# Sparse attention of a two-block network: constant products in front of the first scores, two weight splits moved into the pieces, and VectorE's work reordered

## The reference, cut to what matters

```python
q, k, v, qi, ki, wi = split(h @ w_in)                # 16 query heads, 4 key heads, index queries/keys
q, k, qi, ki = partial_rope(...)                      # rotary part: 16 of 64 features
score = einsum(relu(qi . ki), wi)                     # index scores, float32
sel = top_k(score where visible, 64)                  # 64 keys for each token
s = (q . k[sel]) / 8 ;  p = softmax(s) ;  o = p . v[sel]
x = x + o @ w_out
```

## Time and profile before

| what | value |
|---|---|
| median of 3 runs | 1656.52 us (1656.01 to 1660.21) |
| the profiled execution | 1656.1 us |
| its span | 1654.0 us |
| mean granted clock | 0.977 |
| busy share: PE, PEld, DVE, ACT | 97%, 93%, 61%, 46% |
| chain that ended last, by engine | PE 84%, DVE 8%, ACT 3%, DMA 3% |

### The profile page before, as it was taken

How to read it: one execution, slowest core, us unless ns; L and a number is a source line. 1 busy time by engine, 2 the same in 40 slices (tenths; PEclk the granted TensorE clock), 3 DMA queues, 4 the chain that set the end, 5 groups by cost and what they waited for, 6 DMA issues and landing times.

```text
span 1654.0 us, 30872 instructions
## 1 busy us (share of the span) xinstructions
PE 1606.0 (97%) x12599; PEld 1535.9 (93%) x12599; DVE 1004.1 (61%) x1233; ACT 764.8 (46%) x1009; POOL 23.1 (1%) x40
## 2 busy tenths in 40 slices
PE   7989999998999999999999999999999999999999
PEld 5868999998899998999987999989999898889998
DVE  6763665557666546656458666466664656676653
ACT  4333554446655534433436444344443435554443
POOL 0000000004000000000000000000000000000000
PEclk9956999999999999999999999999999999999999
DMA  5610666655056665555731557635566353146673
GB/s 167 166 61 1 178 190 189 184 169 156 27 169 190 193 186 166 178 166 178 199 117 52 180 177 202 178 102 180 177 203 178 102 181 100 57 142 185 201 210 96
DMA packets 339943, 253.62 MB, mean 153 GB/s; under 512 B 16302, under 2 KB 338700, under 8 KB 339868
## 3 DMA queue, kind: packets, MB, share of 16 engines
q1 hardware_dynamic: 337104, 250.00, 51.2%
q10 hardware_dynamic: 2764, 2.56, 0.6%
HBM read 250.51 MB, written 1.05 MB: 152 GB/s over the span
## 4 chain that ended last, share of the span: by engine, by line
PE 84%; DVE 8%; ACT 3%; DMA 3%; issue 1%; ACTq 0%; SPq 0%; DVEq 0%
PE acc L560 25%; PE acc L562 24%; PE acc L561 24%; DVE w_low L1774 2%; ACT w_high L1238 2%; PE acc L792 2%; PE spare L760 2%; PE acc L778 1%; PE acc L585 1%; DMA w_raw<-in_mlp_w_down_dram 1%; DMA w_raw<-in_ffn_w_dram 1%; DVE x_state L1984 1%; DVE xg_low L1818 1%; DVE evac_a L1982 1%; PE spare L623 1%
## 5 line engine op out<-in xcount | busy, mean ns | idle before, releaser
L1774 DVE TENSOR_TENSOR w_low<-w_raw,w_high 128x2048 fp32r<-128x2048 f32 (+2 forms) x218 | 519.5, 2383 | 373.2 <-ACT w_high L1238 373.1
L1238 ACT ACTIVATE w_high<-w_raw 128x2048 fp32r<-128x2048 f32 (+2 forms) x218 | 433.7, 1990 | 592.8 <-PE acc L562 553.9
L560 PE MATMUL acc<-xg_high,w_high 128*128 128x272 f32 (+2 forms) x2320 | 662.2, 285 | 7.7 <-DVE xg_low L1818 4.4
L562 PE MATMUL acc<-xg_high,w_low 128*128 128x272 f32 (+2 forms) x2320 | 654.7, 282 | 0.0
L561 PE MATMUL acc<-xg_low,w_high 128*128 128x272 f32 (+2 forms) x2320 | 654.7, 282 | 0.0
L560 PEld LDWEIGHTS acc<-xg_high,w_high 128*128 128x128 f32 (+1 forms) x2320 | 435.4, 188 | 19.4 <-issue 9.5
L561 PEld LDWEIGHTS acc<-xg_low,w_high 128*128 128x128 f32 (+1 forms) x2320 | 435.4, 188 | 1.2 <-issue 0.5
L562 PEld LDWEIGHTS acc<-xg_high,w_low 128*128 128x128 f32 (+1 forms) x2320 | 435.5, 188 | 0.2
L560 PE MATMUL acc<-hidden_high,w_high 128*128 128x256 f32 (+1 forms) x1216 | 342.5, 282 | 4.1 <-DVE w_low L1774 4.0
L561 PE MATMUL acc<-hidden_low,w_high 128*128 128x256 f32 (+1 forms) x1216 | 341.5, 281 | 0.0
L562 PE MATMUL acc<-hidden_high,w_low 128*128 128x256 f32 (+1 forms) x1216 | 341.5, 281 | 0.0
(11 more groups left out here) (307 smaller groups left out, 1482.9 us busy)
## 6 DMA issues: line engine op xcount, KB each, us to landing
w_raw<-in_ffn_w_dram SPq DMA_DIRECT2D x88, 1024.0 KB, 5.3
w_raw<-in_ffn_w_dram SPq DMA_DIRECT2D x32, 1408.0 KB, 7.0
w_raw<-in_mlp_w_up_dram SPq DMA_DIRECT2D x32, 1024.0 KB, 5.7
w_raw<-in_mlp_w_down_dram SPq DMA_DIRECT2D x32, 1024.0 KB, 5.7
w_raw<-in_attn_w_qkv_dram SPq DMA_DIRECT2D x12, 1024.0 KB, 5.0
w_raw<-in_a_w_in_dram SPq DMA_DIRECT2D x4, 1024.0 KB, 7.5
w_raw<-in_a_w_in_dram SPq DMA_DIRECT2D x8, 512.0 KB, 5.2
w_raw<-in_a_w_out_dram SPq DMA_DIRECT2D x4, 1024.0 KB, 5.2
```

Of the source, the lines that this page charges most:

```text
L560: pe.matmul(dst, high_w, high, start=first, stop=False)
L562: return pe.matmul(dst, low_w, high, start=False, stop=last)
L1238: act.activation(whi[slot(c)][:, 0:SIZES[c]], raw[c % 2][:, 0:SIZES[c]], ACT.Copy).then_inc(S["w_high"], 1)
L1774: dve.tensor_tensor(wlo[slot(c)][:, s], raw[c % 2][:, s], whi[slot(c)][:, s].bitcast(F32), ALU.subtract)\
```

## The change

On TensorE, three constant products of 512 columns stand in front of piece 0's scores, before the wait for the keys, and three more in front of piece 4's, before the wait for the last heads. The wait for the score bank now comes ahead of these, and the hook gets the piece's number. The constant products inside pieces 0 and 1 go from two and one to four each. The two splits of `a_out`'s first chunks leave the input projection: ScalarE does them behind the exponentials of pieces 4 and 6, VectorE behind the maxima of pieces 6 and 7. On VectorE, the rotation of the keys comes ahead of the second half's weighing, unit 8 is scaled after one more round of selection and not after four, and the rotation of the last heads moves from piece 1 to piece 0.

```diff
--- before.py
+++ after.py
@@ -752,10 +752,10 @@
                     return mask is not None and pieces[p][0] == 0
 
                 def make_scores(p):
-                    if before is not None:
-                        before(*pieces[p])
                     if p >= 2:
                         pe.wait_ge(*((S["exp_done"], e0 + p - 1) if masked(p - 2) else (S["s_read"], s0 + p - 1)))
+                    if before is not None:
+                        before(p)
                     for c, (q, k) in enumerate(scores(*pieces[p])):
                         ins = pe.matmul(sp[p % 2][:, c, 0:k.shape[1]], q, k, start=True, stop=not masked(p))
                     if not masked(p):
@@ -897,11 +897,13 @@
             pe.wait_ge(S["idx_relu"], 8)
             pe.wait_ge(S["tables_ready"], 1)
 
-            def heads_ready(i, m):
-
-                if i == 0 and m == 0:
+            def heads_ready(p):
+
+                if p == 0:
+                    keep_busy(sp[0][:, 0], 3)
                     pe.wait_ge(S["key_back"], 16 * 4)
-                if i == 0 and m == 4:
+                if p == 4:
+                    keep_busy(sp[0][:, 0], 3)
                     pe.wait_ge(S["query_back"], 16 * 4)
 
             def halves(i):
@@ -913,7 +915,7 @@
                                      qkA[c * HD:(c + 1) * HD, 4 + 5 * (m // 4), 0:(i + 1) * P]) for c in range(2)],
                       halves,
                       lambda i, m, c, kt, nk: vA[:, kt, (2 * (m // 4) + c) * HD:(2 * (m // 4) + c + 1) * HD],
-                      "exp_done", [2] + [1] * 7, 4, before=heads_ready,
+                      "exp_done", [4, 4] + [1] * 6, 4, before=heads_ready,
                       mask=((S["hide_ready"], 1), identA[:], hide[:, 0, 0:P], 0, P))
             turn_out("o_read", n.get("o_read"))
             keep_busy(acc[0][:, 0], 2)
@@ -1531,15 +1533,15 @@
             split(g.c0 + 8)
             pack(6, first_heads, packK, "key_packed")
             relus(4)
-            split(g.c0 + 9)
             unpack(first_heads, packK, "key_roped", "key_back")
-            split(g.c0 + 10)
             pack(8, last_heads, packQ, "query_packed")
 
             def beside_exps(p):
 
                 if p == 1:
                     unpack(last_heads, packQ, "query_roped", "query_back")
+                if p in (4, 6):
+                    split(g.c0 + 7 + p // 2)
 
             attention([(i, m) for i in range(2) for m in range(8)], lambda i: (i + 1) * P,
                       lambda i: [(0, 2 * (i + 1), P)], None, sp, beside_exps)
@@ -2212,8 +2214,10 @@
 
             def second_block(p):
 
-                if p == 1:
+                if p == 0:
                     rope_packed(packQ, "query_packed", "query_roped")
+                if p in (6, 7):
+                    split(g.c0 + 3 + p)
                 if p < 6:
                     take_eight(1, 2 if p < 2 else 1)
                 if p == 5:
@@ -2244,14 +2248,12 @@
             projected(6, qkA[:, 2:4, :], 2, A_SCALE)
             split(g.c0 + 8)
             take_eight(0, 3)
+            rope_packed(packK, "key_packed", "key_roped")
             weigh(4)
-            rope_packed(packK, "key_packed", "key_roped")
             projected(7, qkA[:, 5:7, :], 2, A_SCALE)
-            split(g.c0 + 9)
+            take_eight(0, 1)
+            projected(8, qkA[:, 7:9, :], 2, A_SCALE)
             take_eight(0, 4)
-            projected(8, qkA[:, 7:9, :], 2, A_SCALE)
-            split(g.c0 + 10)
-            take_eight(0, 1)
             hide_rest(0)
             pieces = [(i, m) for m in range(8) for i in range(2)]
```

## The result

| | before | changed |
|---|---|---|
| median of 20 executions each, timed together | 1655.80 us (1641.44 to 1661.52) | 1645.75 us (1633.41 to 1655.49) |
| ratio, 95% interval | | 0.9943 [0.9916, 0.9969] |
| profiled execution, span | 1656.1, 1654.0 us | 1645.72, 1643.6 us |
| first product of `a_out` | 154.77 | 145.82 |

A forecast was written before the change was run, and what follows sets the result against it. TensorE was taken to bind the kernel, with sparse attention at half clock. First scores 1.7 plus 21 at full clock gave 22.7 us, less 1.8 given back: -20.9 from 1656.1, stated as 1635.5 us, range 1631 to 1652.

The forecast's parts named there:

- First scores: Start of the sparse attention: unit 8 scaled earlier, scores at 84.8 in place of 86.53, 1.7 us earlier.
- Pieces 0 to 3: Sparse attention's first pieces: added constants hidden at full clock, piece 4's scores at 99.9 in place of 101.23.
- Rival 2: Clock lost in pieces 1 to 3 and not brought back by the constants: 1657 us; chance 0.07.
- The pieces at full clock: Sparse pieces from 4 on at 1.00: short 1.55, long about 2.0, then tail, turning and constants end at 132.0; 21 us gained.
- rival 1: Clock falls again at the splits in pieces 6 and 7: only 7.3 us gained, 1649 us; chance 0.27.
- Given back: Later in the kernel: shifted idle times cause one more clock fall, costing 1.8 us.
- Rival 3: MLA's attention does not get its clock back: about 20 us more; chance 0.10.
- Rival 4: Path held by DMAs or VectorE: only the first scores' 1.7 us stay, 1654 us; chance 0.04.
- Loads: Third and fourth chunk of `a_out` load later, at about 107 and 110, 5.2 us, hidden by some 16 us.
- The Trainium skill's rule on turnings: Full clock "doesn't engage" for transpose mode, so pieces would lose what constants win; the prediction held MLA's trace against it.

The follow-up runs named there:

- filled at the splits: Changed kernel with 6 for 1 constant products of 128 columns ahead of piece 7's turning and 2 ahead of piece 8's; 1633.28 us, 0.9892 of the kernel before.
- at the start: Changed kernel with 8 for 4 constant products of 128 columns ahead of piece 0's turning, none added beside the splits; 1640.24 us, 0.9946 of the kernel before.
- without constants: Changed kernel without its added constant products, moved splits and VectorE's new order kept; 1645.71 us, 0.9975 of the kernel before.

## Why the prediction was wrong

**First scores: right.** 85.24 for 84.8; constants begin at 82.43 for 82.2.

**Pieces 0 to 3: right.** Piece 4 at 99.67 for 99.9. The hole at 91 to 95 is deep enough to lose the clock in some executions (at 94 in three of the profiles here), but with the three constants ahead of piece 4 it was back by 100.3 at the latest. Rival 2 did not come.

**The pieces at full clock: the prices right, the condition wrong.** Piece 10's scores came at 111.72 for 112.3, though a short piece took 1.68 for 1.55 (its mask products 0.37 for 0.3), and VectorE's second split waited 0.17 us for ScalarE's, which the prediction had through 0.1 ahead of it; where the clock holds, a long piece takes 2.06 for 2.0, piece 15 is at 123.09 for 122.3, and `a_out` starts at 133.25 for 132.0, at the end behind VectorE's 2.50 us of `out_low`. Of 30 executions of the changed kernel 14 lie at 1632.82 to 1641.95 (median 1637.0, the forecast within 1.5) and 16 at 1643.38 to 1655.49 (median 1649.2). The gap between the groups is narrow, but the mean granted clock puts the border at the same place: 0.991 or more in the 14, 0.990 or less in the 16. One execution of each group was profiled. The second group is rival 1 (its 1649, with the first product at 145.82 for 147.4), given 0.27; it took 16 of 30. The step that failed is "In pieces 6 and 7 TensorE has about 1.55 us of work in 3.0", taken as enough in most cases. TensorE was not thin there: from 99 to 109 it was busy 9.89 of 10.00 us, since it still had scores to make ahead, up to piece 9's. The waiting stood together behind that, from 109 to 113, where the division and piece 8's first use of the mask on VectorE add to piece 7's split: 2.47 of 4.00 us. The runs filled at the splits and at the start show that this stretch, and not the one at 90 to 93, is where the long pieces lose the clock.

**The base: the second step that failed.** The prediction read one profiled execution as the kernel before ("Once at 0.50, this layer did not recover in 52 us"). Of its 99 executions in all, 48 lie at 1637.34 to 1648.27 (median 1644.0) and 51 at 1651.15 to 1663.98 (median 1656.5); in one of the former it did recover, after 27 us. The forecast's 20.9 set a changed kernel of the lower group against a kernel before of the upper, which are 19.5 us apart (1656.5 to 1637.0). Group against group the change gives 7.0 (1644.0 to 1637.0) and 7.3 (1656.5 to 1649.2) us. That the latter is rival 1's "7.3 less" to the tenth is partly luck: between the two profiles the first product moved 8.95. The median of one batch moves by up to 9 us with how many executions fall in each group (the kernel before: 1655.80, 1647.69, 1646.63 and 1651.65).

The Trainium skill's page "TensorE: Matmul & The Clock Gate", Part 1, says that the clock's monitor runs freely, so that the same kernel shows a different number of slow products from run to run. The traces agree: unchanged, the kernel before had its falls at 85.4 and 95.6, at 84.2 and 97.9, and at 85.8 and 96.0. The page puts the ramp at under 1% of a typical span; the 12.5 us between the groups of the kernel before are 0.8% of this one, and more than the change.

**Given back.** No added fall in MLA here: two spared and one added, 1.4 us gained for 1.8 lost. Rival 3, MLA's attention at half clock, is real but not the change's doing: the kernel before had it from 393 to 410 in one execution. Rival 4 is out.

**Loads.** `a_out`'s third and fourth chunks now load from about 108 to 114.5 (DMA share 0.99 from 109 to 113) and nothing on the chain waits for them: hidden, as forecast.

**The Trainium skill's rule on turnings** (Part 4 of the same page), weighed in the prediction, does not hold for these: long pieces, about a third of them turnings, kept 1.00 from 113.3 to 133.0, and sixteen turnings in a row (3.68 us at 0.50) were followed by full clock at 144.0, ahead of any constant product.

## What to carry to other kernels

Before changing what holds TensorE's clock, profile the kernel several times and sort its times: with two groups, a forecast made against one execution can be wrong by the distance between them. When work is moved onto an engine that paces TensorE, look for the thinnest few microseconds that it leaves, also behind the moved work, and fill these with constant products that no one waits for: seven more of 128 columns were worth as much as leaving VectorE's splits out (0.9892 and 0.9906 of the kernel before). Constants must stand ahead of the wait that makes the hole; behind it they ran at half clock here and cost their full length, 5.46 us for 2.81.

## What was not expected of the hardware

- With TensorE busy 26.64 of 27.00 us, and 33.65 of 34.10, the clock stayed at 0.50; once four constant products of 512 columns were put in, it was 1.00 two us after the first of them began (one profile). TensorE being busy at half clock was not enough here to bring the clock back.
- Still the long pieces' own products brought it back in some executions: of the kernel before at 123.3 in one profile, and among the last products with the values at 142.1 and 142.3 in two, at 139.8 without constants. In the two others of the kernel before it came back at 153.6, behind the turnings.
- The same 4.00 us, with 2.47 of them busy, were followed by half clock in one execution of the changed kernel and by full clock in another.
- The same program on the same chip spreads over 24 us (1640.21 to 1663.98). The mean granted clock goes with it, 0.989 against 0.972; as an estimate that is up to 28 us of full clock (0.017 of the time), enough for the whole spread.
